# Two additive biases moved from VectorE and GpSimd into TensorE's accumulation, in a kernel of two transformer blocks

## The chip, the cores and the metric

The kernel runs on one core of a Trainium2 chip. The core has a matrix engine (TensorE, PE in the profile, whose weight loads stand in rows of their own as PEld), three engines for element work (VectorE or DVE, ScalarE or ACT, GpSimd or POOL), a queue engine that here only starts transfers (SyncE or SP), and 16 DMA engines. Each engine runs its own stream of instructions in order, and the streams meet at semaphores. The metric is the device time of one execution in microseconds: 2225.22 us, the median of 3 runs of the kernel before (2223.93 to 2225.47).

## The reference

256 tokens of width 2048 pass through two blocks in float32. Only two places of the first and second block matter here. In the first block a third of the mixer is a spatial gating unit: six heads, whose normalised values are mixed over the positions of a chunk of 128 and get a bias per head and position before they gate `u`:

```python
v = layernorm(v, ln_g, ln_b).reshape(B, L // CHUNK, CHUNK, N_GMLP_HEADS, GMLP_HEAD_DIM)
g = jnp.einsum('bnpec,eqp->bnqec', v, w_s) + b_s.T[:, :, None]
return u * g.reshape(B, L, D_GMLP)
```

The second block has causal attention of 16 heads of 128, with a bias on the logits that comes from forget gates, `cum[t]` being the running sum of their logarithms:

```python
log_f = jax.nn.log_sigmoid((f_pre + b_f).astype(jnp.float32)).transpose(0, 2, 1)
cum = jnp.cumsum(log_f, axis=-1)
logits = jnp.einsum('bhqd,bhkd->bhqk', q_i, k).astype(jnp.float32) * scale
logits = logits + c_i[..., :, None] - cum[..., None, :]
logits = jnp.where(pos_k[None, :] <= pos_q[:, None], logits, -jnp.inf)
p = jax.nn.softmax(logits, axis=-1)
```

The rest is eight large products with weight matrices (projections in and out, two feed-forward networks) with norms, convolutions and an FFT-like mixer between them.

## The kernel before

The weights come in 374 units of 1 MB. SP loads each into one of four buffers `raw` (L310). ACT rounds it to the short format fp32r into `whi` (L398), DVE subtracts to get the rest, `wlo` (L687); both have three buffers. PE multiplies each unit with the activations, which are split in the same way: 16 matmuls of 512 columns with `whi` (L1357) and 16 of 256 columns with `wlo` (L1368) for a unit of an input projection; 8 pairs with `whi` (L1392, L1393) and 8 with `wlo` (L1397) for a unit of an output projection. The units of the gated values and of the attention's values use L1360, L1361 and L1370. What DVE and ACT write beside, they write in the shadow of these products.

The order is written out by hand. A table `SIDE` says which small pieces of work an engine does behind which unit, and the engines go through the same table. `group` on ACT and DVE puts the pieces between the splits of the coming units; PE does them behind the unit's last matmul (`side(u)`).

The two places of the change:

**The gating unit.** `mix(j)`, j = 0 to 5. PE multiplies the normalised values of head j with its position matrix, once for each chunk of 128 (L1234), into one of the banks 4 to 7. DVE adds the bias from `bsb`, a row that a DMA has copied to all 128 partitions (L355), and writes `mb` (L832), then multiplies by the activated `u` into `actT` (L836). Heads 0 and 1 stand behind units 31 and 32, heads 2 and 3 behind unit 33, and heads 4 and 5 (`LAST_MIX`) right behind them. The next PE work is `rows(0)`, the output projection, whose first matmuls go to banks 4 and 5 and so wait until DVE has read heads 4 and 5 out of them. The last two blocks of `u` leave PE with unit 33 and pass through ACT (L441), DVE (L1083, L1086) and ACT's gelu (L605).

**The attention.** `sums` stands behind unit 194: PE multiplies the gate logarithms with a triangular matrix, once for the sums by head (L1326) and once by token (L1329); DVE copies them out as `cT` (16 heads by 256 positions, L912) and `ctok` (L914). POOL writes `cT` to DRAM (L366), reads it back into all 128 partitions by four DMAs (L369), and adds the causal mask for each head into `cbs` (L378, L379). `scores(h)` stands behind units 196, 200, up to 224, two heads at a time: PE multiplies queries and keys (L1249), the first 128 queries with 128 keys and the second 128 queries with 256. DVE adds `ctok` of the query and `cbs` of the key in one instruction per part (L928, L929) and takes the maximum (L931, L932); ACT does the exponential (L526, L527).

The kernel's functions that the change touches:

Of the kernel before, what the change touches and what calls it, by code (L numbers as in the profile page):

```python
# [120 lines left out]
def two_block_program(nc, A, out, cum):  # L121
    with ExitStack() as ctx:
        def sb(name, shape, dt=F):
            return ctx.enter_context(nc.sbuf_tensor(name, shape, dt))
# [18 lines left out]
        edge = sb("edge", [P, 64])  # L143
        bank = [ctx.enter_context(nc.psum_tensor(f"bank{i}", [P, 512], F)) for i in range(8)]
# [10 lines left out]
        def piece(q):  # L155
# [29 lines left out]
        bsb = view(5120, HY)  # L185
        mb = view(5888, 512, 2, T)
# [7 lines left out]
        qk = view(8192, 2048, 8, T)  # L194
        Sx = view(10496, 1536, 4, 384)
# [5 lines left out]
        cbs = view(17728, 768, 2, 384)  # L201
# [46 lines left out]
        s_gv, s_mean, s_nsq, s_napp, s_mix, s_mixb, s_mixd, s_gu, s_gelu, s_pg, s_pm, s_pd = (  # L248
            sem(n) for n in ("s_gv", "s_mean", "s_nsq", "s_napp", "s_mix", "s_mixb", "s_mixd", "s_gu", "s_gelu", "s_pg", "s_pm", "s_pd"))
# [3 lines left out]
        s_gf, s_xout, s_v, s_gt, s_ga, s_cum, s_cumd, s_qk0, s_qk, s_cbm, s_sc, s_scd, s_ex, s_dv, s_tp, s_pt, s_pv, s_pvt = (  # L253
            sem(n) for n in ("s_gf", "s_xout", "s_v", "s_gt", "s_ga", "s_cum", "s_cumd", "s_qk0", "s_qk", "s_cbm", "s_sc",
# [74 lines left out]
        def gpsimd(e):  # L329
# [25 lines left out]
            e.dma_start(bsb, A["gm_b_row"].partition_broadcast(P)).then_inc(s_bs, 16)  # L355
# [322 lines left out]
        def vector(e):  # L678
# [231 lines left out]
            def sums():  # L910
                e.wait_ge(s_cum, 2)
                e.tensor_scalar(cT, bank[5][0:16, 0:T], -1.0, None, ALU.mult).then_inc(s_cumd, 1)  # L912
                e.wait_ge(s_cum, 6)
                e.tensor_copy(ctok.rearrange("p (h c) -> p h c", h=2),  # L914
                              bank[4][:, 0:64].rearrange("p (h c) -> p h c", h=2)[:, :, 0:NH]).then_inc(s_cumd, 1)

            def scores(h):
                s, b = Sx[:, h % 4, :], 4 + h % 2
                mx = st[:, 22 + 2 * (h % 2):24 + 2 * (h % 2)]
                e.wait_ge(s_sc, h + 1)  # L920
                e.wait_ge(s_cumd, 2)
                e.wait_ge(s_cbm, 2 * h + 2)
                cb = cbs[:, h % 2, :]
# [4 lines left out]
                e.scalar_tensor_tensor(s[:, 0:P], bank[b][:, 0:P], ctok[:, h:h + 1], cb[:, 0:P], ALU.add, ALU.add).then_inc(s_scd, 1)  # L928
# [264 lines left out]
        def tensor(e):  # L1193
# [235 lines left out]
            rows(0, [in_free(18, 0), in_free(18, 1), in_free(17, 0), in_free(17, 1), (s_mixb, 5), (s_mixb, 6), (s_mixb, 3), (s_mixb, 4)])  # L1429
# [146 lines left out]
```

## Time and profile before

| | |
|---|---|
| median of 3 runs | 2225.22 us |
| the profiled execution | 2225.47 us |
| its span, first to last instruction | 2223.6 us |
| mean granted TensorE clock | 0.996 |
| PE busy | 2182.6 us, 98% of the span |
| PEld busy | 1871.3 us, 84% |
| DVE, ACT, POOL busy | 1306.7, 1013.5, 50.9 us |
| read from memory | 406.12 MB, 184 GB/s over the span |

The profile is of one execution. Busy time is the sum of an engine's instructions; the ends of matmuls are modelled, so a busy PE isn't one at its peak, and the distance between the starts of matmuls tells more than their length. One float32 matmul stands in the trace as two records, one fp32r matmul as one; both read "f32" in PE's rows.

### The profile page before, as it was taken

Reading aid. Unit: us, or ns where it says so; the run is one execution under the profiler, and the core shown is the slowest. Engines: PE = TensorE matmul, PEld = TensorE weight load, DVE = VectorE, ACT = ScalarE, POOL = GpSimd, SP = SyncE. Lnnn points to the kernel's source line nnn. Section 1 sums busy time; section 2 is a strip of 40 time slices with the busy share of each in tenths; the row PEclk is TensorE's granted clock in tenths of the full one; section 3 lists DMA queues with packets and bytes.
Section 4 is the critical chain, followed back from the end, with each engine's and each line's share of the span. In section 5 each row is a group of like instructions: output and inputs, shape, how many; then the busy total and the mean of one; then the engine's idle time right before and its main releaser. Section 6 shows DMA issues by size and latency. Waiting matters only on the chain.

```text
span 2223.6 us, 28008 instructions
## 1 busy us (share of the span) xinstructions
PE 2182.6 (98%) x11702; PEld 1871.3 (84%) x11702; DVE 1306.7 (59%) x1596; ACT 1013.5 (46%) x1227; POOL 50.9 (2%) x75
## 2 busy tenths in 40 slices
PE   7999999999999999999999999989999999999998
PEld 6888788888888888888898889878888888888886
DVE  7757647777777775444655665456555555444444
ACT  5444436545454554334654444444333334333333
POOL 1030000000000000000001000000000000000000
PEclk9999999999999999999999999999999999999999
DMA  9554555655555555555566555546666665555552
GB/s 303 159 159 152 197 189 177 210 189 187 188 188 188 188 189 189 190 190 187 155 191 200 161 171 190 190 132 192 188 188 189 190 189 189 190 189 189 189 189 95
DMA packets 267869, 410.04 MB, mean 184 GB/s; under 512 B 6629, under 2 KB 246309, under 8 KB 249312
## 3 DMA queue, kind: packets, MB, share of 16 engines
q1 hardware_dynamic: 264672, 395.47, 54.3%
q0 software_dynamic: 2352, 11.47, 1.4%
q8 instruction: 92, 1.51, 0.3%
q10 hardware_dynamic: 720, 1.32, 0.2%
q14 instruction: 33, 0.27, 0.0%
HBM read 406.12 MB, written 2.11 MB: 184 GB/s over the span
## 4 chain that ended last, share of the span: by engine, by line
PE 93%; DVE 2%; ACT 2%; issue 1%; DMA 1%; DVEq 0%; SPq 0%; ACTq 0%
PE bank L1357 33%; PE bank L1368 17%; PE bank L1392 11%; PE bank L1397 11%; PE bank L1393 11%; PE bank L1360 2%; PE bank L1361 2%; PE bank L1370 2%; DMA raw<-in_w_in 1%; ACT whi L398 1%; DVE wlo L687 1%; PE bank L1249 1%; PE bank L1203 1%; ACT M L416 0%; DVE M L1138 0%
## 5 line engine op out<-in xcount | busy, mean ns | idle before, releaser
L687 DVE TENSOR_TENSOR wlo<-raw,whi 128x2048 fp32r<-128x2048 f32 (+1 forms) x374 | 857.1, 2293 | 807.9 <-ACT whi L398 807.9
L398 ACT ACTIVATE whi<-raw 128x2048 fp32r<-128x2048 f32 (+1 forms) x374 | 715.8, 1916 | 823.8 <-PE bank L1397 442.8
L1357 PE MATMUL bank<-hh,whi 128*128 128x512 f32 x3392 | 825.4, 396 | 15.0 <-ACT whi L398 11.1
L1357 PEld LDWEIGHTS bank<-hh,whi 128*128 128x128 f32 x3392 | 626.6, 189 | 146.9 <-ACT whi L398 11.1
L1368 PEld LDWEIGHTS bank<-hh,wlo 128*128 128x128 f32 x3392 | 429.9, 188 | 17.3
L1368 PE MATMUL bank<-hh,wlo 128*128 128x256 f32 x3392 | 434.9, 281 | 0.0
L1392 PE MATMUL bank<-whi,hh 128*128 128x512 f32 x1088 | 428.8, 394 | 2.2 <-DVE M L832 2.2
L1393 PE MATMUL bank<-whi,hh 128*128 128x512 f32 x1088 | 427.5, 393 | 0.0
L1397 PE MATMUL bank<-wlo,hh 128*128 128x512 f32 x1088 | 274.3, 394 | 0.0
L1392 PEld LDWEIGHTS bank<-whi,hh 128*128 128x128 f32 x1088 | 204.5, 188 | 50.8 <-issue 2.4
L1397 PEld LDWEIGHTS bank<-wlo,hh 128*128 128x128 f32 x1088 | 204.3, 188 | 47.4
L1393 PEld LDWEIGHTS bank<-whi,hh 128*128 128x128 f32 x1088 | 204.5, 188 | 46.5
L459 ACT ACTIVATE M<-M,cols 128x256 f32<-128x256 f32 x106 | 58.0, 595 | 158.1 <-DVE M L768 158.1
L1360 PE MATMUL bank<-whi,hh 128*128 128x258 f32 (+1 forms) x352 | 88.3, 290 | 2.0 <-ACT whi L398 2.0
L1361 PE MATMUL bank<-whi,hh 128*128 128x258 f32 (+1 forms) x352 | 86.6, 285 | 0.0
L441 ACT ACTIVATE M<-bank 128x256 f32<-128x256 f32 x212 | 67.7, 371 | 19.1 <-PE bank L1368 9.6
L1360 PEld LDWEIGHTS bank<-whi,hh 128*128 128x128 f32 x352 | 67.7, 192 | 2.6 <-ACT whi L398 2.2
L1361 PEld LDWEIGHTS bank<-whi,hh 128*128 128x128 f32 x352 | 67.8, 193 | 0.4
L771 DVE SCALAR_TENSOR_TENSOR M<-M,cols 128x255 f32<-128x255 f32 x106 | 51.4, 484 | 18.2 <-ACT M L459 17.8
L754 DVE TENSOR_TENSOR hh<-M,hh 128x256 fp32r<-128x256 f32 x140 | 57.9, 419 | 4.4 <-ACT hh L438 4.4
L438 ACT ACTIVATE hh<-M 128x256 fp32r<-128x256 f32 x140 | 55.2, 400 | 6.6 <-PE bank L1368 3.4
L774 DVE SCALAR_TENSOR_TENSOR M<-M,cols 128x255 f32<-128x255 f32 x106 | 46.3, 479 | 0.0
(217 smaller groups left out, 893.1 us busy)
## 6 DMA issues: line engine op xcount, KB each, us to landing
raw<-in_mlp_w SPq DMA_DIRECT2D x128, 1024.0 KB, 5.4
raw<-in_ffn_w_up SPq DMA_DIRECT2D x88, 1024.0 KB, 5.0
raw<-in_ffn_w_down SPq DMA_DIRECT2D x44, 1024.0 KB, 4.7
raw<-in_w_in SPq DMA_DIRECT2D x34, 1024.0 KB, 5.5
raw<-in_fox_w_in SPq DMA_DIRECT2D x32, 1024.0 KB, 5.3
raw<-in_fox_w_in SPq DMA_DIRECT2D x16, 1032.0 KB, 5.5
raw<-in_w_out SPq DMA_DIRECT2D x16, 1024.0 KB, 4.8
raw<-in_fox_w_out SPq DMA_DIRECT2D x16, 1024.0 KB, 4.7
```

The costliest lines, as they stand in the source:

```text
L398: e.activation(whi[i % RING][:, 0:n], raw[i % RAW][:, 0:n], ACT.Copy).then_inc(s_hi, 1)
L441: return e.activation(dst, bank[b][:, T:2 * T], ACT.Copy)
L459: e.activation(dst, src, ACT.Identity, bias=bias, scale=ws[1]).then_inc(s_cv1, 1)
L687: e.tensor_tensor(wlo[i % RING][:, 0:n], raw[i % RAW][:, 0:n], whi[i % RING][:, 0:n].bitcast(F), ALU.subtract).then_inc(s_lo, 1)
L754: e.tensor_tensor(hlo[:, row_slot(stage, k), :], src[:, c, :], hhi[:, row_slot(stage, k), :].bitcast(F), ALU.subtract).then_inc(s_alo, 1)
L1357: e.matmul(bank[b][:, :], wh[:, k, s], hh[:, kk, :], start=kk == 0, stop=False)
L1360: e.matmul(o, hhi[:, kk, s], wh[:, k, :], start=kk == 0, stop=False)
L1361: e.matmul(o, hlo[:, kk, s], wh[:, k, :], start=False, stop=False)
L1368: t = e.matmul(bank[b][:, T:2 * T], wl[:, k, s], hhi[:, kk, :], start=False, stop=kk == KD - 1)
L1392: e.matmul(bank[b][:, :], hhi[:, s, h * P:h * P + P], wh[:, 512 * j:512 * j + 512], start=k == 0, stop=False)
L1393: e.matmul(bank[b][:, :], hlo[:, s, h * P:h * P + P], wh[:, 512 * j:512 * j + 512], start=False, stop=False)
L1397: t = e.matmul(bank[b][:, :], hhi[:, s, h * P:h * P + P], wl[:, 512 * j:512 * j + 512], start=False, stop=False)
```

## The change

The gating bias becomes a second matmul into the same bank: for each head and chunk PE multiplies a row of 128 ones (one partition) with the head's 128 biases (`bs6`, one partition, loaded by one small DMA), in float32. DVE's addition, `mb`, `bsb` and their semaphore go. Banks 4 to 7 are now free when DVE's multiplication by the activated `u` has been done.

The attention's key bias becomes a matmul too. DVE splits `cT` into an fp32r part and its rest and stacks them in `cs2`, partitions 0 to 15 and 32 to 47 of 64, which POOL has zeroed. For each head POOL multiplies `cs2` by a column `sel` that is one at the head's two rows and zero elsewhere, into `nck` (two buffers, fp32r); PE multiplies 64 rows of ones with it, 128 and 256 columns, behind each product of queries and keys. The way through DRAM and POOL's 32 additions go; DVE's additions read the mask itself. `sel` adds 16 columns to the packed constants.

```diff
@@ POOL @@
-            e.dma_start(bsb, A["gm_b_row"].partition_broadcast(P)).then_inc(s_bs, 16)
+            e.dma_start(bs6, A["gm_b_s"]).then_inc(s_bs, 16)
...
-            e.wait_ge(s_cumd, 1)
-            e.dma_start(cum[:, :], cT).then_inc(s_cdram, 16)
-            e.wait_ge(s_cdram, 16)
-            for n in range(4):
-                e.dma_start(actT[:, 4 * n:4 * n + 4, :].rearrange("p h t -> p (h t)"),
-                            cum[4 * n:4 * n + 4, :].rearrange("h t -> (h t)").partition_broadcast(P)).then_inc(s_cb[n], 16)
-            e.wait_ge(s_fox, 48)
+            e.memset(cs2, 0.0).then_inc(s_zero, 1)
+            e.wait_ge(s_cumd, 5)
             for h in range(NH):
-                b = cbs[:, h % 2, :]
-                if h % 4 == 0:
-                    e.wait_ge(s_cb[h // 4], 16)
                 if h >= 2:
-                    e.wait_ge(s_scd, 4 * (h - 2) + 2)
-                e.tensor_tensor(b[:, 0:P], actT[:, h, 0:P], msk[:, P:T], ALU.add).then_inc(s_cbm, 1)
-                e.tensor_tensor(b[:, P:384], actT[:, h, :], msk, ALU.add).then_inc(s_cbm, 1)
+                    e.wait_ge(s_sc, h - 1)
+                e.tensor_scalar(nck[:, h % 2, :], cs2, col("sel", h, 64), None, ALU.mult).then_inc(s_nck, 1)
@@ DVE, the gating unit @@
             def mix(j):
                 e.wait_ge(s_mix, j + 1)
-                e.wait_ge(s_bs, 16)
-                if j >= 2:
-                    e.wait_ge(s_mixd, j - 1)
-                e.tensor_tensor(mb[...], bank[4 + j % 4][:, 0:T]..., bsb[...]..., ALU.add).then_inc(s_mixb, 1)
-                e.wait_ge(s_mixb, j + 1)
                 e.wait_ge(s_gelu, j + 1)
-                e.tensor_tensor(actT[:, 10 + j, :], mb[:, j % 2, :], actT[:, 10 + j, :], ALU.mult).then_inc(s_mixd, 1)
+                e.tensor_tensor(actT[:, 10 + j, :], bank[4 + j % 4][:, 0:T], actT[:, 10 + j, :], ALU.mult).then_inc(s_mixd, 1)
@@ DVE, the attention @@
             def sums():
                 e.wait_ge(s_cum, 2)
                 e.tensor_scalar(cT, bank[5][0:16, 0:T], -1.0, None, ALU.mult).then_inc(s_cumd, 1)
+                e.wait_ge(s_cumd, 1)
+                e.tensor_copy(nck[0:16, 0, :], cT).then_inc(s_cumd, 1)
+                e.wait_ge(s_cumd, 2)
+                e.wait_ge(s_zero, 1)
+                e.tensor_copy(cs2[0:16, :], nck[0:16, 0, :].bitcast(F)).then_inc(s_cumd, 1)
+                e.tensor_tensor(cs2[32:48, :], cT, nck[0:16, 0, :].bitcast(F), ALU.subtract).then_inc(s_cumd, 1)
...
-                e.scalar_tensor_tensor(s[:, P:384], bank[b][:, P:384], ctok[:, NH + h:NH + h + 1], cb[:, P:384], ALU.add, ALU.add).then_inc(s_scd, 1)
+                e.scalar_tensor_tensor(s[:, P:384], bank[b][:, P:384], ctok[:, NH + h:NH + h + 1], msk, ALU.add, ALU.add).then_inc(s_scd, 1)
@@ PE @@
             def mix(j):
-                e.wait_ge(*((s_pd, j + 1) if j < 4 else (s_mixb, j - 3)))
+                e.wait_ge(*((s_pd, j + 1) if j < 4 else (s_mixd, j - 3)))
...
                 for n in range(2):
-                    t = e.matmul(bank[b][:, n * P:n * P + P], V[:, n, j * P:j * P + P], wsT[:, j, :], start=True, stop=True)
-                t.then_inc(s_mix, 1)
+                    o = bank[b][:, n * P:n * P + P]
+                    e.matmul(o, V[:, n, j * P:j * P + P], wsT[:, j, :], start=True, stop=False)
+                    t = e.matmul(o, ones[0:1, :], bs6[0:1, j * P:j * P + P], start=False, stop=True)
+                    if n:
+                        t.then_inc(s_mix, 1)
             def scores(h):
-                if h < 2:
-                    e.wait_ge(s_cumd, 2)
+                e.wait_ge(s_nck, h + 1)
...
                     w = P * (i + 1)
-                    t = e.matmul(bank[b][:, P * i:P * i + w], qT[:, i * P:i * P + P], kT[:, 0:w], start=True, stop=True)
-                t.then_inc(s_sc, 1)
+                    o = bank[b][:, P * i:P * i + w]
+                    e.matmul(o, qT[:, i * P:i * P + P], kT[:, 0:w], start=True, stop=False)
+                    t = e.matmul(o, onesr[0:64, :], nck[:, h % 2, 0:w], start=False, stop=True)
+                    if i:
+                        t.then_inc(s_sc, 1)
...
-            rows(0, [..., (s_mixb, 5), (s_mixb, 6), (s_mixb, 3), (s_mixb, 4)])
+            rows(0, [..., (s_mixd, 5), (s_mixd, 6), (s_mixd, 3), (s_mixd, 4)])
```

Three places show how the instructions stand. The first is PE at the end of the input projection, heads 4 and 5 of the gating unit and the start of the output projection; X holds the normalised values, M the activations and biases, hh the split activations. Before:

```order
L1234 MATMUL bank4<-X 128x128 [waits s_mixb]
L1234 MATMUL bank4<-X 128x128
L1234 MATMUL bank5<-X 128x128 [waits s_mixb]
L1234 MATMUL bank5<-X 128x128
L1392 MATMUL bank4<-whi1,hh 128x512 [waits s_mixb,s_alo,s_hi]
L1393 MATMUL bank4<-whi1,hh 128x512
L1392 MATMUL bank5<-whi1,hh 128x512 [waits s_mixb]
```

And after:

```order
L1224 MATMUL bank4<-X 128x128 [waits s_mixd]
L1225 MATMUL bank4<-M,ones 128x128
L1224 MATMUL bank4<-X 128x128
L1225 MATMUL bank4<-M,ones 128x128
L1224 MATMUL bank5<-X 128x128 [waits s_mixd]
L1225 MATMUL bank5<-M,ones 128x128
L1224 MATMUL bank5<-X 128x128
L1225 MATMUL bank5<-M,ones 128x128
L1386 MATMUL bank4<-whi1,hh 128x512 [waits s_mixd,s_alo,s_hi]
L1387 MATMUL bank4<-whi1,hh 128x512
L1386 MATMUL bank5<-whi1,hh 128x512 [waits s_mixd]
```

Each product is followed by one with the ones, and the output projection's first matmul in banks 4 and 5 waits for DVE's multiplication instead of its addition.

The second place is DVE at the same point, from heads 2 and 3 to heads 4 and 5. Before:

```order
L832 TENSOR_TENSOR M<-bank,M 128x256 [waits s_mixd,s_bs,s_mix]
L836 TENSOR_TENSOR M<-M 128x256 [waits s_gelu,s_mixb]
L1083 TENSOR_TENSOR M<-bank,M 128x256 [waits s_gus,s_unit]
L1083 TENSOR_TENSOR M<-bank,M 128x256 [waits s_gus]
L1086 TENSOR_TENSOR M<-M,rb 128x256 [waits s_gu] x2
L832 TENSOR_TENSOR M<-bank,M 128x256 [waits s_mixd,s_bs,s_mix]
L836 TENSOR_TENSOR M<-M 128x256 [waits s_gelu,s_mixb]
```

And after:

```order
L820 TENSOR_TENSOR M<-bank,M 128x256 [waits s_gelu,s_mix] x2
L1071 TENSOR_TENSOR M<-bank,M 128x256 [waits s_gus,s_unit]
L1071 TENSOR_TENSOR M<-bank,M 128x256 [waits s_gus]
L1074 TENSOR_TENSOR M<-M,rb 128x256 [waits s_gu] x2
L820 TENSOR_TENSOR M<-bank,M 128x256 [waits s_gelu,s_mix] x2
```

One instruction per head is left, and it waits for PE and for the gelu together.

The third place is PE at the first two heads of the attention, behind unit 196. Before:

```order
L1249 MATMUL bank4<-M 128x128 [waits s_cumd,s_qk]
L1249 MATMUL bank4<-M 128x256
L1249 MATMUL bank5<-M 128x128 [waits s_cumd,s_qk]
L1249 MATMUL bank5<-M 128x256
L1357 MATMUL bank0<-hh,whi2 128x512 [waits s_hi]
```

And after:

```order
L1241 MATMUL bank4<-M 128x128 [waits s_nck,s_qk]
L1242 MATMUL bank4<-nck,ones 128x128
L1241 MATMUL bank4<-M 128x256
L1242 MATMUL bank4<-nck,ones 128x256
L1241 MATMUL bank5<-M 128x128 [waits s_nck,s_qk]
L1242 MATMUL bank5<-nck,ones 128x128
L1241 MATMUL bank5<-M 128x256
L1242 MATMUL bank5<-nck,ones 128x256
```

Four matmuls for two heads have become eight, and the first of each head waits for POOL's `nck`.

## Rows read from the trace of the kernel before

**Rows 1.** The page: busy time by engine, and PE's clock in 40 slices.

```profile
PE 2182.6 (98%) x11702; PEld 1871.3 (84%) x11702; DVE 1306.7 (59%) x1596; ACT 1013.5 (46%) x1227; POOL 50.9 (2%) x75
...
PEclk9999999999999999999999999999999999999999
```

**Rows 2.** PE's waits over the span: who waited for whom, us, times, longest.

```profile
PE bank L1357 <- ACT whi L398: 11.1, 1, 11.1
...
PE bank L1392 <- DVE M L832: 2.2, 1, 2.2
```

**Rows 3.** PE in order of time around unit 196: start, length, line, operation.

```profile
1179.69 2.05 PE L1368 MATMUL bank<-hh,wlo 128*128 128x256 f32 x16
1181.57 1.48 PE L1249 MATMUL bank<-M 128*128 128x128 f32 x8
1182.70 4.01 PE L1357 MATMUL bank<-hh,whi 128*128 128x512 f32 x16
1186.55 2.04 PE L1368 MATMUL bank<-hh,wlo 128*128 128x256 f32 x16
1188.43 3.87 PE L1357 MATMUL bank<-hh,whi 128*128 128x512 f32 x16
```

**Rows 4.** The same at `sums`, behind unit 194.

```profile
1168.26 1.04 PE L1326 MATMUL bank<-M 128*16 128x256 f32 x4
1169.22 1.07 PE L1329 MATMUL bank<-M 128*128 128x16 f32 x8
1170.14 0.37 PE L1360 MATMUL bank<-whi,hh 128*128 128x258 f32 x1
```

**Rows 5.** The gating unit's end in order of time, on PE, DVE and ACT.

```profile
249.73 1.95 PE L1234 MATMUL bank<-X 128*128 128x128 f32 x16
...
250.38 0.42 DVE L832 TENSOR_TENSOR M<-bank,M 128x256 f32<-128x256 f32 x1 [1.21 <-PE bank L1234]
...
251.63 0.42 DVE L836 TENSOR_TENSOR M<-M 128x256 f32<-128x256 f32 x1
251.97 0.75 DVE L1083 TENSOR_TENSOR M<-bank,M 128x256 f32<-128x256 f32 x2
...
253.09 0.75 ACT L605 ACTIVATE M<-M 128x256 f32<-128x256 f32 x2 [2.50 <-DVE M L1086]
253.30 0.42 DVE L832 TENSOR_TENSOR M<-bank,M 128x256 f32<-128x256 f32 x1
253.87 0.47 PE L1392 MATMUL bank<-whi,hh 128*128 128x512 f32 x1 [2.19 <-DVE M L832]
...
254.57 0.51 PE L1392 MATMUL bank<-whi,hh 128*128 128x512 f32 x1
```

**Rows 6.** All instructions of the gating products, by line and form: count, busy us, mean ns.

```profile
L1234 PE MATMUL bank<-X 128*128 128x128 f32 x24 | 3.2, 274 | 0.0
```

**Rows 7.** DVE in order of time at `sums`.

```profile
1169.33 0.41 DVE L912 TENSOR_SCALAR M<-bank 16x256 f32<-16x256 f32 x1 [2.43 <-PE bank L1326]
1170.33 0.19 DVE L914 COPY M<-bank 128x32 f32<-128x32 f32 x1 [0.58 <-PE bank L1329]
```

**Rows 8.** POOL in order of time: the mixer's slowest operation, then the attention's bias.

```profile
153.75 3.07 POOL L350 TENSOR_TENSOR M<-M 128x384 f32<-128x384 f32 x1
1173.02 2.12 POOL L369 DMA_DIRECT2D M<-cum  x4 [2.48 <-DMA cum<-M]
1180.78 0.73 POOL L379 TENSOR_TENSOR M<-M 128x256 f32<-128x256 f32 x1
```

**Rows 9.** Waits between 1165 and 1365 us, all engines.

```profile
DVE M L928 <- PE bank L1249: 6.8, 8, 1.9
PEld bank L1249 <- DVE M L1119: 1.0, 4, 0.3
```

**Rows 10.** The start of the program on ACT, in order of time.

```profile
5.78 1.71 ACT L406 ACTIVATE hh<-X,cols 128x256 fp32r<-128x256 f32 x4 [3.10 <-DMA cols<-in_cols]
9.12 1.91 ACT L398 ACTIVATE whi<-raw 128x2048 fp32r<-128x2048 f32 x1 [1.63 <-DMA raw<-in_w_in]
```

More of the change, by code:

```diff
@@ L36 @@
 for _name, _n in (("mix", 16), ("ffn", 16), ("g0", 16), ("g2", 16), ("hyw", 54), ("hyb", 18), ("skip", 6),
-                  ("poolb", 4), ("pools", 4), ("ffw", 264), ("ffb", 88), ("gf", 16), ("filt", 4)):
+                  ("poolb", 4), ("pools", 4), ("ffw", 264), ("ffb", 88), ("gf", 16), ("sel", 16), ("filt", 4)):
     COLS[_name] = _at
@@ L118, in row_slot, with two_block_program @@
     return (k - ROWS[stage][1]) % 16
-def two_block_program(nc, A, out, cum):
+def two_block_program(nc, A, out):
     with ExitStack() as ctx:
@@ L143, in two_block_program @@
         edge = sb("edge", [P, 64])
+        nck = sb("nck", [64, 2, T], R)
         bank = [ctx.enter_context(nc.psum_tensor(f"bank{i}", [P, 512], F)) for i in range(8)]
@@ L184, in two_block_program @@
         wsT = Xf[:, 3072:3840].rearrange("p (e q) -> p e q", e=6)
-        bsb = view(5120, HY)
-        mb = view(5888, 512, 2, T)
+        bs6 = M[0:1, 5120:5888]
         fact = view(0, 44 * T, 44, T)
@@ L194, in two_block_program @@
         qk = view(8192, 2048, 8, T)
+        cs2 = M[0:64, 10240:10496]
         Sx = view(10496, 1536, 4, 384)
@@ L200, in two_block_program @@
         cT = M[0:16, 17408:17664]
-        cbs = view(17728, 768, 2, 384)
         ctok = view(17664, 2 * NH)
@@ L230, in two_block_program @@
             sem(n) for n in ("s_col", "s_id", "s_const", "s_decay", "s_fscale", "s_edge", "s_ln", "s_bs", "s_again", "s_fox"))
-        s_outd, s_outp, s_cdram = sem("s_outd"), sem("s_outp"), sem("s_cdram")
-        s_cb = [sem(f"s_cb{n}") for n in range(4)]
-        s_ones, s_pad = sem("s_ones"), sem("s_pad")
+        s_outd, s_outp = sem("s_outd"), sem("s_outp")
+        s_ones, s_pad, s_zero = sem("s_ones"), sem("s_pad"), sem("s_zero")
         s_hx, s_lx, s_sq, s_sumd, s_tot = (sem(n) for n in ("s_hx", "s_lx", "s_sq", "s_sumd", "s_tot"))
@@ L246, in two_block_program @@
         s_cv0, s_cvr, s_cv1, s_cv2, s_z, s_silu, s_fact = (sem(n) for n in ("s_cv0", "s_cvr", "s_cv1", "s_cv2", "s_z", "s_silu", "s_fact"))
-        s_gv, s_mean, s_nsq, s_napp, s_mix, s_mixb, s_mixd, s_gu, s_gelu, s_pg, s_pm, s_pd = (
-            sem(n) for n in ("s_gv", "s_mean", "s_nsq", "s_napp", "s_mix", "s_mixb", "s_mixd", "s_gu", "s_gelu", "s_pg", "s_pm", "s_pd"))
+        s_gv, s_mean, s_nsq, s_napp, s_mix, s_mixd, s_gu, s_gelu, s_pg, s_pm, s_pd = (
+            sem(n) for n in ("s_gv", "s_mean", "s_nsq", "s_napp", "s_mix", "s_mixd", "s_gu", "s_gelu", "s_pg", "s_pm", "s_pd"))
         s_ahi, s_alo, s_row, s_xsum = (sem(n) for n in ("s_ahi", "s_alo", "s_row", "s_xsum"))
-        s_gf, s_xout, s_v, s_gt, s_ga, s_cum, s_cumd, s_qk0, s_qk, s_cbm, s_sc, s_scd, s_ex, s_dv, s_tp, s_pt, s_pv, s_pvt = (
-            sem(n) for n in ("s_gf", "s_xout", "s_v", "s_gt", "s_ga", "s_cum", "s_cumd", "s_qk0", "s_qk", "s_cbm", "s_sc",
+        s_gf, s_xout, s_v, s_gt, s_ga, s_cum, s_cumd, s_qk0, s_qk, s_nck, s_sc, s_scd, s_ex, s_dv, s_tp, s_pt, s_pv, s_pvt = (
+            sem(n) for n in ("s_gf", "s_xout", "s_v", "s_gt", "s_ga", "s_cum", "s_cumd", "s_qk0", "s_qk", "s_nck", "s_sc",
                              "s_scd", "s_ex", "s_dv", "s_tp", "s_pt", "s_pv", "s_pvt"))
@@ L920, in scores @@
                 e.wait_ge(s_sc, h + 1)
-                e.wait_ge(s_cumd, 2)
-                e.wait_ge(s_cbm, 2 * h + 2)
-                cb = cbs[:, h % 2, :]
+                e.wait_ge(s_cumd, 5)
                 if h >= 4:
@@ L927, in scores @@
                     e.wait_ge(s_ex, 2 * h - 2)
-                e.scalar_tensor_tensor(s[:, 0:P], bank[b][:, 0:P], ctok[:, h:h + 1], cb[:, 0:P], ALU.add, ALU.add).then_inc(s_scd, 1)
-                e.scalar_tensor_tensor(s[:, P:384], bank[b][:, P:384], ctok[:, NH + h:NH + h + 1], cb[:, P:384], ALU.add, ALU.add).then_inc(s_scd, 1)
+                e.scalar_tensor_tensor(s[:, 0:P], bank[b][:, 0:P], ctok[:, h:h + 1], msk[:, P:T], ALU.add, ALU.add).then_inc(s_scd, 1)
+                e.scalar_tensor_tensor(s[:, P:384], bank[b][:, P:384], ctok[:, NH + h:NH + h + 1], msk, ALU.add, ALU.add).then_inc(s_scd, 1)
                 e.wait_ge(s_scd, 4 * h + 2)
@@ L1428, in tensor @@
                 mix(j)
-            rows(0, [in_free(18, 0), in_free(18, 1), in_free(17, 0), in_free(17, 1), (s_mixb, 5), (s_mixb, 6), (s_mixb, 3), (s_mixb, 4)])
+            rows(0, [in_free(18, 0), in_free(18, 1), in_free(17, 0), in_free(17, 1), (s_mixd, 5), (s_mixd, 6), (s_mixd, 3), (s_mixd, 4)])
             def up_free(g, n):
@@ L1542 @@
     ng = g["norm_g_2"][0]
+    sel = np.zeros((P, NH), np.float32)
+    sel[0:NH] = sel[32:32 + NH] = np.eye(NH)
     rows64 = np.zeros((P, 4), np.float32)
@@ L1548 @@
         cols(g["hy_skip"][0]), cols(g["pool_b"][0]), cols(g["pool_scale"][0]), cols(g["ffn_conv_w"][0]), cols(g["ffn_conv_b"][0]),
-        cols(g["norm_final"]), rows64], axis=1)
+        cols(g["norm_final"]), sel, rows64], axis=1)
     filt = np.zeros((64, 128), np.float32)
@@ L1571 @@
     out = nc.dram_tensor("out_0", (P, 2, D), F, kind="ExternalOutput").ap()
-    cum = nc.dram_tensor("cum", (NH, T), F, kind="Internal").ap()
-    two_block_program(nc, aps, out, cum)
+    two_block_program(nc, aps, out)
     r = run_bass_kernel_spmd(nc, [feeds], core_ids=[0])
```

6 lines of the change are left out of this document (2 added, 4 removed).

## The prediction

> **What bounds the kernel now.** I read the busy times first, then what PE waited for, then PE's order of time at the two places of the change. PE is busy for 2182.6 of 2223.6 us at full clock in every slice, the next engine, DVE, for 59% [rows 1]. PE's waits are few and single: 11.1 us at the start, then one or two at a seam between stages; of them only the 2.2 us of L1392 on DVE's L832 lies at a place that the change touches [rows 2]. In the attention's stretch PE's matmuls do not wait, but for four gaps in front of queries times keys that sum to 1.0 us on the weight loads and that DVE's L1119 ends, an instruction the change leaves alone; DVE's logits wait for PE and not for POOL [rows 9]. So PE's own instructions set the end, and whatever is added between them is paid, except where PE stands idle today. Work taken from DVE, POOL or the DMAs pays only where it shortens a PE wait.
>
> The measure for PE is the distance between starts. An fp32r matmul of 256 columns costs (1188.43 - 1186.55) / 16 = 0.1175 us [rows 3]. A float32 matmul is two records: the 12 gating products stand as 24 [rows 6]. Sixteen such records of 128 columns take 1.95 us, the last being 0.27 long, so (1.95 - 0.27) / 15 = 0.112 us each [rows 5]. Records of only 16 columns cost (1170.14 - 1169.22) / 8 = 0.115 us, and those of 256 columns (1169.22 - 1168.26) / 4 = 0.24 us [rows 4]. From 16 to 128 columns nothing changes; below 128 the weight load before each matmul sets the pace, at about 0.112.
>
> **The change part by part.** *The gating bias on PE.* 12 float32 matmuls of 128 columns are added, 24 records of 0.112 us = 2.7 us. Only the 8 records of heads 0 and 1, behind units 31 and 32, stand before units that are ready: 8 x 0.112 = 0.90 us on the path. The 16 records of heads 2 to 5 (1.79 us) stand ahead of PE's idle 2.19 us [rows 5] and fill it, so what they cost is how far that wait's end moves.
>
> *The wait's end.* Today: the products of heads 2 to 5 start at 249.73, DVE takes head 2 at 250.38, is done with head 3 at 251.63 + 0.42, turns to the two blocks of u at 251.97 (the trace lets neighbours overlap a little), ACT's gelu starts 1.12 us later, at 253.09, and the first L832 behind it at 253.30; PE starts bank 4 at 253.87 and bank 5 at 254.57 [rows 5]. After: head 3's last product is the 16th record, not the 8th, and ends near 249.73 + 15 x 0.112 + 0.27 = 251.68. DVE has one instruction for it, 251.73 to 252.15, so the blocks of u start at about 252.17, 0.20 later, and the gelu at 253.29. The multiplication of head 4 must now wait for the gelu of its block: 253.29 + 0.38 + 0.05 = 253.7 to 254.15, with PE 0.15 behind it, at 254.30, and its third matmul, the first in bank 5, two matmuls further, at 254.30 + 0.31 + 0.23 = 254.84 (head 5's multiplication ends at 254.60, before that). Against 254.57 this is +0.27 us. PE's own queue, full until 249.73 + 31 x 0.112 + 0.27 = 253.5, is not the last. Behind PE stands the whole output projection, behind DVE the split of unit 36, which waits for ACT anyway (ACT's split follows the gelu by 0.1 us) and is needed 10 us later.
>
> If heads 2 to 5 were not hidden at all this term would be +1.79; if the saved additions of heads 2 and 3 (0.84 us) moved the wait's end forward in full, -0.6.
>
> *The attention's bias on PE.* For each of 16 heads two fp32r matmuls, of 128 and of 256 columns. The 256-column one is of the same kind as L1368: 0.1175. No row has an fp32r matmul of 128 columns. From below: half of 0.1175, 0.06, if columns alone count. From above: 0.225, the two records of 0.112 that float32 takes, if the short matmul gets no benefit from its format. I take 0.112, the floor that the 16-column records show. Sum 16 x (0.112 + 0.1175) = 3.67 us, with ends 16 x 0.1775 = 2.8 and 16 x 0.3425 = 5.5. All of it is on the path: these stand between two units whose whi and wlo are ready, with no idle time before or behind them [rows 3].
>
> The Trainium skill ("TensorE: Matmul & The Clock Gate", Back-to-back issue gap) gives 81 ns for a sustained matmul of 128 columns with its weight load. The 0.112 of rows 5 contradicts it for float32. By that figure the estimate for all additions would be 8 x 0.081 + 0.27 + 16 x (0.081 + 0.1175) = 4.1 us instead of 4.8.
>
> *DVE, POOL and the wait on nck.* `sums` gets three instructions of 16 partitions by 256. At 0.41 each as L912 [rows 7] plus a semaphore between them, the last ends near 1169.74 + 3 x 0.43 = 1171.0, `ctok` at 1171.2, and the split behind it starts 0.8 us later; its unit is needed near 1182. POOL then makes nck for heads 0 and 1. Nearest rows: 0.73 us for 128x256, up to 3.07 for 128x384 [rows 8]. Even 3.07 each ends by 1177.4, while PE comes to head 0 at 1181.57 [rows 3]. Later pairs have some 25 us. Cost zero, hidden under unit 195 and 196; the cover ends at (1181.57 - 1171.2) / 2 = 5.2 us for each POOL instruction. The trip through DRAM that goes had landed at 1180.0, before PE came: it wins nothing. DVE's logits start later by the two or four added matmuls, 0.46 us for a pair; the exponentials and splits behind them finish more than 4 us before PE's next unit, so this is not seen.
>
> *Constants and DMA.* `cols` grows by 16 of 522 columns, 3% of a transfer that lands before 5.78 us; the first unit's weights, which land at 9.12, gate PE [rows 10]. The removed broadcasts were not waited for by PE. Both zero, within 0.1.
>
> **Sum.** 0.90 + 0.27 + 3.67 = +4.84 us. The profiled execution took 2225.47 us, which is 0.25 above the median of 2225.22; from its own time the sum gives 2230.3, from the median 2230.1. I take 2230.1, +0.22%. What a measurement of this kernel can tell from no change is about 0.2%, here 4.45 us; the forecast is only just over it.
>
> **Rivals.** *A, not slower: the weight load isn't the floor for the new matmuls.* The 64 rows of ones are fp32r; if their load is quicker than a float32 one, the 128-column matmuls stream at 0.06 and the attention's term is 2.84. Sum 0.90 + 0.27 + 2.84 = 4.0, 2229.2 us, +0.18%: no change. For it: no row has an fp32r load that isn't covered by 256 columns. Against: the 16-column floor, and 0.1175 for 256 columns lies above the 0.107 of streaming at 2.4 GHz, so even there something is added for the load. It decides at 0.088 us for the short matmul, where the total is 4.45.
> The Trainium skill (the same page, Weight-path perf modes) says that fast weight load applies to 128 weights of a type other than FP32. If the chip counts fp32r as another type, that is rival A; no row here shows it.
>
> *B: short fp32r matmuls cost as float32.* Then the attention's term is 5.48 and the time 2225.2 + 6.65 = 2231.9, +0.30%. For it: no product of the kernel uses fp32r under 256 columns, so no row excludes it. Against: float32 itself reaches 0.112 for a record of 128 columns, and one record of fp32r has no reason in the rows to take longer than one of float32.
>
> *C: POOL becomes the wait.* If a multiplication by a column takes 8 us for 64 partitions, nck of head 1 comes 16 us after 1171.2 and PE waits 5.6 us once: 2235.7. Against: 3.07 is the longest POOL row.
>
> *D, faster: PE gets its pace back.* If the 2 MB of broadcast and POOL's additions disturbed PE's reads, their removal would speed up the matmuls around. It would need more than 4.84 us of some 180 us of attention. Against: the 256-column matmuls of unit 196, during the broadcast's aftermath and POOL's additions, take (1181.57 - 1179.69) / 16 = 0.1175, as those of unit 197 when neither runs [rows 3]. Where it holds, a time of 2224 or less.
>
> **How the numbers follow.** My forecast has 0.55, A 0.17, B 0.20, C 0.04, D 0.04. Around 4.84 the two added places and the run-to-run spread of a median leave about 0.8 us either way, so the forecast itself gives slower by over 0.2% in two of three cases, 0.36, and no change in 0.19. A gives no change, 0.12, and slower 0.05; B and C slower, 0.24; D no change or faster, half each. Together faster 0.02, no change 0.34, slower 0.64; I shift a little for what no row shows: 0.03, 0.35, 0.62. The range runs from A less its spread, 2227.4, to B plus its spread, 2232.9.
>
> **What would show it.** In the profile after, L1242's records of 128 and 256 columns stand 0.11 and 0.12 us before the next start; a distance of 0.06 is A, of 0.22 is B. The pair of heads behind unit 196 takes 1.13 + 0.46 = 1.6 us from its start to the next unit's. L1225 has 24 records at 0.112. The wait of L1386 on DVE shrinks from 2.19 to about 0.8 us (254.30 against the end of PE's queue at 253.5) and ends 0.4 us later than today, counted from head 2's first product; if it ends 1 us later, that step is wrong. POOL's tensor_scalar is under 1 us and no PE wait names it. I am wrong altogether if PE's waits elsewhere change by more than 1 us.

## The result, and the profile after

The changed kernel takes 2248.2 us in the median of four runs (2247.5 to 2249.1), the kernel before 2225.3 (2223.9 to 2226.6). The ratio is 1.0102, with a 95% interval of 1.0087 to 1.0118: slower by 22.9 us, where 4.9 were forecast. The profiled executions took 2247.4 and 2225.5 us, their spans are 2244.9 and 2223.6 us. The working below is made against these spans, +21.3 us; that is 1.6 less than between the medians, and the four runs of the kernel before alone lie 2.7 us apart.

The page after: busy time by engine, and PE's clock in 40 slices.

```profile
PE 2206.8 (98%) x11758; PEld 1883.9 (84%) x11758; DVE 1306.1 (58%) x1593; ACT 1013.3 (45%) x1227; POOL 46.5 (2%) x55
...
PEclk9999999999999999999999999999999999999999
```

Against [rows 1], PE has 56 records more, as the change has it (24 gating records, 32 attention matmuls), and 24.2 us more busy time. That is 0.43 us for each record, where 0.11 to 0.12 were forecast. DVE and ACT are busy for as long as before, within 0.6 us, and POOL for 4.4 us less.

PE's longest waits in the span after: who waited for whom, us, times, longest.

```profile
PE bank L1351 <- ACT whi L388: 10.9, 1, 10.9
PE bank L1191 <- DVE X L1132: 7.1, 3, 5.0
PE bank L1197 <- DVE M L716: 3.4, 1, 3.4
PE bank L1354 <- ACT whi L388: 2.1, 1, 2.1
PE bank L1351 <- DVE M L755: 1.4, 1, 1.4
```

The 2.2 us of L1392 [rows 2] are gone altogether, and the rest stands as it was, within 0.6 us. So no wait was added: the time is inside PE's own sequence. PE in order of time, at the first pair of heads behind unit 196:

```profile
1189.01 0.39 PE L1241 MATMUL bank<-M 128*128 128x128 f32 x2
1189.32 0.33 PE L1242 MATMUL bank<-nck,ones 64*128 64x128 f32 x1
1189.58 0.70 PE L1241 MATMUL bank<-M 128*128 128x256 f32 x2
1190.21 0.38 PE L1242 MATMUL bank<-nck,ones 64*128 64x256 f32 x1
1190.52 0.49 PE L1241 MATMUL bank<-M 128*128 128x128 f32 x2
1190.94 0.32 PE L1242 MATMUL bank<-nck,ones 64*128 64x128 f32 x1
1191.19 0.70 PE L1241 MATMUL bank<-M 128*128 128x256 f32 x2
1191.82 0.38 PE L1242 MATMUL bank<-nck,ones 64*128 64x256 f32 x1
1192.13 0.74 PE L1351 MATMUL bank<-hh,whi 128*128 128x512 f32 x2
```

The pair took 1.13 us [rows 3] and takes 3.12, not 1.6. The bias matmuls of 64 rows are not the only ones that have become dear: from an L1242 to the next L1241 it is 0.26 to 0.31 us, and the two records of an L1241 of 256 columns behind it take 0.63 us up to the next start, where they took 0.43. The weight loads show what happens, first a pair of before, then the changed kernel (same columns, the bracket is idle time):

```profile
1181.46 1.19 PEld L1249 LDWEIGHTS bank<-M 128*128 128x128 f32 x8
```

```profile
1188.89 0.31 PEld L1241 LDWEIGHTS bank<-M 128*128 128x128 f32 x2
1189.32 0.18 PEld L1242 LDWEIGHTS bank<-nck,ones 64*128 64x128 f32 x1
1189.58 0.30 PEld L1241 LDWEIGHTS bank<-M 128*128 128x128 f32 x2
1190.21 0.18 PEld L1242 LDWEIGHTS bank<-nck,ones 64*128 64x128 f32 x1 [0.33 <-issue]
```

Before, the eight loads of a pair ran one behind the other, beside the matmuls ahead of them. Now the weight load engine is idle ahead of each load of an L1242, and waits for nothing that the profile can name: for 0.12 us behind the loads of a product of 128 columns, for 0.33 us behind those of one of 256 columns. The longer gap comes 16 times and sums to 5.3 us. The gaps stand where the number of weight rows changes, and they are longer where the matmul ahead is longer, as if the load waited for that matmul to end.

The gating products of heads 2 to 5, the same view (rows between repeat):

```profile
252.01 0.39 PE L1224 MATMUL bank<-X 128*128 128x128 f32 x2
252.33 0.48 PE L1225 MATMUL bank<-M,ones 1*128 1x128 f32 x2
252.74 0.49 PE L1224 MATMUL bank<-X 128*128 128x128 f32 x2
253.16 0.48 PE L1225 MATMUL bank<-M,ones 1*128 1x128 f32 x2
...
258.60 0.79 PE L1225 MATMUL bank<-M,ones 1*128 1x128 f32 x2
259.32 0.80 PE L1386 MATMUL bank<-whi,hh 128*128 128x512 f32 x1
```

Four records cost 0.83 us instead of 4 x 0.112 = 0.45: 0.19 more for each of the two changes. From head 2 to the output projection it was 4.14 us with 2.19 of them idle [rows 5]; now it is 7.31 with none. And at the end the clock falls. Windows, before the fall and in it (length; busy time with count of PE, PEld, DVE, ACT, POOL; granted clock; DMA share; GB/s):

```profile
252.00:257.30 5.30, 5.30 (x28) 3.74 (x26) 2.18 (x6) 1.16 (x4) 0.00 (x0) 1.00 0.40 165
257.50:263.10 5.60, 5.60 (x15) 4.16 (x15) 3.20 (x4) 2.15 (x3) 0.55 (x1) 0.50 0.37 102
```

From 257.5 us the clock is at half, 1.2 GHz, for 6.8 us, right behind a stretch in which PE was busy all the time at 2.4 GHz.

Where the 21.3 us are: I set the starts of ACT's splits, unit by unit, against those of before. The difference is -0.25 at unit 34 (the start), 7.5 from unit 37 on, flat to unit 198, 22.6 at unit 228 and 21.2 from unit 250 on. So the gating brings 7.7 us, the attention 15.1, and at the seam behind it 1.3 come back: there the clock is at half in one piece of 6.8 us that PE waits through in part (busy 4.8), and not in two of 3.4 (busy 6.5 together). By an estimate, half of the busy time at half clock is lost, 2.4 against 3.2 us, and PE's wait on DVE's hh is 0.6 us shorter. So these 1.3 us go with where the clock falls and not with the new matmuls; the runs set side by side under "The gating part again" bear this out.

### The profile page after: what moved, and what is told of

Its sections match the earlier page's. It is cut to its first block, busy times and chain, and to the rows that moved or that the text cites. A ratio compares the mean times of both kernels' runs of the same rounds, so it can differ in the third digit from the quotient of the medians.

```text
span 2244.9 us, 28087 instructions
## 1 busy us (share of the span) xinstructions
PE 2206.8 (98%) x11758; PEld 1883.9 (84%) x11758; DVE 1306.1 (58%) x1593; ACT 1013.3 (45%) x1227; POOL 46.5 (2%) x55
## 4 chain that ended last, share of the span: by engine, by line
PE 94%; DVE 2%; ACT 2%; issue 1%; DMA 1%; DVEq 0%; SPq 0%; ACTq 0%
PE bank L1351 33%; PE bank L1362 17%; PE bank L1386 11%; PE bank L1391 11%; PE bank L1387 11%; PE bank L1354 2%; PE bank L1355 2%; PE bank L1364 2%; DMA raw<-in_w_in 1%; ACT whi L388 1%; DVE wlo L677 1%; PE bank L1241 1%; PE bank L1191 0%; PE bank L1242 0%; ACT M L406 0%
## 5 line engine op out<-in xcount | busy, mean ns | idle before, releaser
L1351 PE MATMUL bank<-hh,whi 128*128 128x512 f32 x3392 | 825.1, 396 | 14.0 <-ACT whi L388 10.9
L1351 PEld LDWEIGHTS bank<-hh,whi 128*128 128x128 f32 x3392 | 626.5, 189 | 145.9 <-ACT whi L388 10.9
L1386 PE MATMUL bank<-whi,hh 128*128 128x512 f32 x1088 | 430.6, 396 | 0.0
L1386 PEld LDWEIGHTS bank<-whi,hh 128*128 128x128 f32 x1088 | 205.5, 189 | 48.6 <-issue 0.2
L431 ACT ACTIVATE M<-bank 128x256 f32<-128x256 f32 x212 | 67.7, 371 | 20.3 <-PE bank L1362 10.9
```

The costliest lines, as they stand in the source:

```text
L431: return e.activation(dst, bank[b][:, T:2 * T], ACT.Copy)
L1351: e.matmul(bank[b][:, :], wh[:, k, s], hh[:, kk, :], start=kk == 0, stop=False)
L1386: e.matmul(bank[b][:, :], hhi[:, s, h * P:h * P + P], wh[:, 512 * j:512 * j + 512], start=k == 0, stop=False)
```

## The experiments

In what follows "H" is the theory that each change of the number of weight rows that the array works with makes PE wait for the matmul ahead before it loads, and "T" that small-row matmuls are slow in themselves. "S" blames the second matmul into the same region of a bank, and "F" the change between float32 and fp32r. Offsets are those of ACT's splits against before, as above.

**One part at a time.** The gating part alone (e1), the attention part alone (e2), each by giving back the other part's lines of before:

```
 e1:  t = e.matmul(bank[b][:, P*i:P*i + w], qT[...], kT[:, 0:w], start=True, stop=True)    # as before
 e2:  t = e.matmul(bank[b][:, n*P:n*P + P], V[...], wsT[:, j, :], start=True, stop=True)   # as before
```

> Only the gating part of the change, the attention as before. Theory H (a change of the number of weight rows between neighbouring matmuls, 128 to 1 and back, lets PE finish and load before it goes on, some 0.2 us each way): 1.1 us more for each of heads 0 and 1, about 2.7 us for heads 2 to 5 beyond the wait they fill, and about 3.4 us of half clock behind them: +7 to +8 us. Rival S (a second matmul into the same bank region right behind the first is what waits): the same here, +7 to +8.

> Only the attention part, the gating unit as before. All theories: 8 pairs of heads at 1.9 us more each, +15 us, less about 1.3 us that the seam behind the attention gave back in the changed kernel: +14 us.

e1: 2233.07 us, ratio 1.0029 (1.0019 to 1.0039). In its profiled run the offset goes from -0.3 to 8.9 at the gating and stays, above the 7 to 8 expected; the clock is at half from 255.6 us for 10.2 us, longer than in the whole change. e2: 2241.85 us, 1.0066 (1.0051 to 1.0081); from -0.1 at unit 198 to 15.1 at unit 228, 13.8 behind the seam. Against the 2226.35 us of before beside them that is 6.7 and 15.5 us in the medians, 22.2 together, where the whole change has 22.9: as far as these medians can tell, the parts add up and don't work on each other.

**The same with 128 rows.** In e3 the gating bias, in e4 the attention bias is multiplied on all 128 rows, the rows added being zeros. Number and length of matmuls stay. e9 is the whole change in this form.

```
-  t = e.matmul(o, ones[0:1, :], bs6[0:1, j * P:j * P + P], start=False, stop=True)
+  t = e.matmul(o, ones, bs6[:, j * P:j * P + P], start=False, stop=True)        # e3, e9
-  t = e.matmul(o, onesr[0:64, :], nck[:, h % 2, 0:w], start=False, stop=True)
+  t = e.matmul(o, onesr[0:128, :], nck[:, h % 2, 0:w], start=False, stop=True)  # e4, e9
```

> As the gating part alone, but the ones and the biases have 128 rows, row 0 the biases and the others zero, so that every matmul has 128 weight rows; same count, columns and format. Theory H: each record back to 0.112 us, no fall of the clock, +0.9 for heads 0 and 1 and up to 0.3 at the wait: +1.2 us. Rival S (same bank region) : unchanged, +7 to +8. Rival F (float32 next to something else) can't apply, both are float32.

> As the attention part alone, but cs2, sel, nck and the ones have 128 rows, the added ones zero. Theory H: the 128-column matmul at 0.112 and the 256-column one at 0.1175, +0.46 us for a pair of heads, +3.7 us in all. Rival F (the alternation of float32 and fp32r is what waits): unchanged, +14. Rival S (same bank region): unchanged, +14.

> The whole change with 128 rows for every matmul of the ones, in both places (zeros below the rows in use). Theory H: the sum that the prediction made for matmuls without any change of row count, +1.0 at the gating unit and +3.7 in the attention, +4.7 us, 2230 us. If something else of the change cost time, it would lie above +6.

e3: 2225.76 us, ratio 0.9998 (0.9989 to 1.0008); the medians can't tell 1 us from nothing, so the order of time has to. The gating adds 1.04 us, from -0.47 to +0.57. PE in order of time at its end:

```profile
253.31 0.39 PE L1231 MATMUL bank<-X 128*128 128x128 f32 x2
253.54 0.39 PE L1232 MATMUL bank<-M,ones 128*128 128x128 f32 x2
254.72 0.47 PE L1391 MATMUL bank<-whi,hh 128*128 128x512 f32 x1 [0.79 <-DVE M L831]
```

The distance is 0.223 for two records, 0.112 each; PE waits 0.79 us where 0.8 were forecast; the clock does not fall. The second matmul into the same region of a bank is still there, so S falls.

e4: 2230.99 us, 1.0015 (1.0006 to 1.0025); 3.76 us from unit 198 to 228, forecast 3.67. The products are float32 and the biases fp32r, as in e2, so F falls too. e9: 2230.78 us against 2225.58, 1.0022 (1.0013 to 1.0031), which is the forecast's 1.0022. Its offset rises by 1.0 at the gating and 3.7 in the attention, and PE stands in the pair so:

```profile
1182.52 0.39 PE L1243 MATMUL bank<-M 128*128 128x128 f32 x2
1182.66 0.30 PE L1244 MATMUL bank<-nck,ones 128*128 128x128 f32 x1
1182.81 0.65 PE L1243 MATMUL bank<-M 128*128 128x256 f32 x2
...
1184.29 2.02 PE L1353 MATMUL bank<-hh,whi 128*128 128x512 f32 x8
```

1.77 us, where the 64 rows took 3.12. Rows of zeros make the kernel faster by 17 us: the count of matmuls was priced rightly, and what was missed hangs on the row number alone.

**How many rows.** e5 takes 96 rows, e6 takes 32 (the low part of the key's bias is left out, since it doesn't fit).

```
-  t = e.matmul(o, onesr[0:64, :], nck[:, h % 2, 0:w], ...)
+  t = e.matmul(o, onesr[0:96, :], nck[:, h % 2, 0:w], ...)     # e5;  onesr[0:32, :] in e6
```

> The attention part alone, with cs2, sel, nck and the ones on 96 rows instead of 64 (the rows above 48 are zero); gating as before. Theory H1 (what matters is the part of the array that a matmul occupies, and 96 rows occupy all of it as 128 do): +3.7 us in the attention, pairs of heads at +0.46. Theory H2 (any difference in the number of rows makes PE finish first): as with 64 rows, +15 us, pairs at +1.9.

> The attention part alone on 32 rows; the low part of the key bias is left out for that (rows 32 to 47 don't exist), so the logits miss it. H1 and H2: a third size of the occupied part, again different from 128, +15 us. A theory in which the price falls or grows with the rows missing: 64 rows cost 1.43 us per pair over the matmuls themselves; 96 missing rows instead of 64 would make it 2.1 and the total about +21 us.

e5: 2229.25 us against 2226.77, 1.0012 (1.0002 to 1.0023), 3.65 us in the attention: as with 128. e6: 2241.23 us, 1.0067 (1.0047 to 1.0087), 15.3 us: as with 64. PE in order of time in e5:

```profile
1182.84 0.39 PE L1244 MATMUL bank<-M 128*128 128x128 f32 x2
1182.98 0.31 PE L1245 MATMUL bank<-nck,ones 96*128 96x128 f32 x1
...
1184.61 0.64 PE L1354 MATMUL bank<-hh,whi 128*128 128x512 f32 x2
```

So not every other number of rows has a price. 96 is as good as 128; 64 and 32 cost, both the same. This fits an array that is used in another division for 64 rows or fewer; the division itself stands in no row.

**Fewer changes, same matmuls.** In e7 two heads are done together, the four products first and then their biases, so that a pair has 4 changes and not 8. The order, with the waits ahead of a pair that it needs, is the only difference to e2.

```
+  for k, q, kk in ((h, qT, kT), (h + 1, qk[:, sl + 1, :], qk[:, sl + 3, :])):
+      e.matmul(bank[4 + k % 2][...], q[...], kk[:, 0:w], start=True, stop=False)
+  for k in (h, h + 1):
+      t = e.matmul(bank[4 + k % 2][...], onesr[0:64, :], nck[:, k % 2, 0:w], start=False, stop=True)
```

> The attention part alone with 64 rows, the two heads of a pair interleaved: two products of queries and keys, then two with the ones, twice. The same matmuls, but 4 changes of the row count per pair instead of 8. Theory H (each change costs some 0.18 us, whatever stands between): 0.46 + 4 x 0.18 = 1.2 us per pair, +9.4 us in the attention. Rival T (each 64-row matmul is slow in itself, 0.36 us each): unchanged, 1.9 per pair, +15 us.

2237.85 us, 1.005 (1.0033 to 1.0066); 11.8 us in the attention. T, which wanted 15, falls; but 9.4 isn't met either. PE in order of time at the first and the second pair of heads:

```profile
1181.32 0.61 PE L1246 MATMUL bank<-M 128*128 128x128 f32 x4
1181.86 0.43 PE L1248 MATMUL bank<-nck,ones 64*128 64x128 f32 x2
1182.22 1.13 PE L1246 MATMUL bank<-M 128*128 128x256 f32 x4
1183.28 0.51 PE L1248 MATMUL bank<-nck,ones 64*128 64x256 f32 x2
1183.72 0.50 PE L1357 MATMUL bank<-hh,whi 128*128 128x512 f32 x1
...
1208.62 0.71 PE L1246 MATMUL bank<-M 128*128 128x128 f32 x4 [0.38 <-DVE M L1114]
```

The first pair takes 2.40 us: 1.77 + 4 x 0.16. The rest is a side effect of the edit: both heads' queries and keys must now be there before the first starts, and PE waits for DVE's copy L1114 (the L1119 of before) 11 times, 4.6 us in all, where it was 4 times and 1.0. I summed the distance from a pair's first product to the next unit's first matmul over the eight pairs:

| kernel | changes | distance, us | over e4, per change |
|---|---|---|---|
| before | 0 | 9.50 | |
| e4, 128 rows | 0 | 14.69 | |
| e5, 96 rows | 0 | 14.72 | |
| e7, 64 rows, in fours | 32 | 19.89 | 0.163 |
| e6, 32 rows | 64 | 25.45 | 0.168 |
| after, 64 rows | 64 | 25.48 | 0.169 |

The price for each change is the same in all three, and T falls on this table alone: the same matmuls take 5.6 us less with half the changes. From unit to unit, as the offsets count, a change costs a little more, 0.177 us; the rest comes in the unit behind. With 3.7 + 32 x 0.163 and 2 to 3.6 us of added waiting (part of it ran beside matmuls still queued) e7 should show 10.9 to 12.5; it shows 11.8.

**The kernel before had the same cost.** Its filter products at L1282 have 64 rows. e10 puts them on 128, with zeros, in the kernel before:

```
-  t = e.matmul(bank[b][:, 0:384], fe[:, m*P:m*P + P], w3[:, ...], start=True, stop=True)                    # M[0:64, ...]
+  t = e.matmul(bank[b][:, 0:384], M[:, 17664 + m*P:17664 + m*P + P], M[:, 9728 + ...], start=True, stop=True)
```

> The kernel before, untouched but for the filter's third product: its weights and data get 128 rows instead of 64, the added ones zero (16 records in two blocks, so 4 changes of the row count go). Theory H: about 0.2 us for each change, -0.8 us in two steps of 0.4 behind units 7 and 10, too little for the time of the whole to show. If the rows of the kernel before were slow there for another reason: no step.

2224.68 us, 0.9994 (0.9986 to 1.0003): too little for a median. But the order of time shows it. Before, then e10, around the first of two such blocks, with the unit behind it:

```profile
59.84 2.08 PE L1368 MATMUL bank<-hh,wlo 128*128 128x256 f32 x16
61.85 2.84 PE L1282 MATMUL bank<-M 64*128 64x384 f32 x8
64.63 2.56 PE L1357 MATMUL bank<-hh,whi 128*128 128x512 f32 x10
...
68.39 2.04 PE L1368 MATMUL bank<-hh,wlo 128*128 128x256 f32 x16
```

```profile
59.58 2.08 PE L1373 MATMUL bank<-hh,wlo 128*128 128x256 f32 x16
61.51 2.74 PE L1287 MATMUL bank<-M 128*128 128x384 f32 x8
63.98 3.26 PE L1362 MATMUL bank<-hh,whi 128*128 128x512 f32 x13
...
67.76 2.05 PE L1373 MATMUL bank<-hh,wlo 128*128 128x256 f32 x16
```

e10 is ahead by 0.26 us in front of the block, and by 0.63 behind it: 0.37 for two changes. Behind the second block it is 1.03, and it stays about there up to unit 36. Four changes, 0.19 each, in another stage, another type of work and without the change under study.

**Everything but the bias matmuls.** e8 leaves both kinds of bias matmul out and keeps all the rest of the change.

```
-  e.matmul(o, V[...], wsT[:, j, :], start=True, stop=False)
-  t = e.matmul(o, ones[0:1, :], bs6[0:1, ...], start=False, stop=True)
+  t = e.matmul(o, V[...], wsT[:, j, :], start=True, stop=True)      # likewise the one on nck
```

> The changed kernel with the matmuls of the ones left out in both places, so that both biases are missing from the output; DVE, POOL and the DMAs are as changed. What the rest of the change is worth: all theories expect the PE wait at the output projection to end some 0.5 us earlier, since DVE's additions are gone, and nothing else: -0.5 us, no change. If freed DVE, POOL or DMA work gave PE back some of its pace (the former rival D), it would be faster by more than 1 us.

2224.96 us, 0.9994 (0.9984 to 1.0003). The offset falls by 0.8 us between units 35 and 36, where 0.5 were expected and the wait on DVE shrinks from 2.2 to 1.7, and is flat in the attention. What DVE, POOL and the DMAs were relieved of pays there and nowhere else.

**The gating part again.** e11 is e1 once more, for the clock.

> The gating part alone once more, one look for the clock. If the drawn-out matmuls of heads 2 to 5 bring the clock down, the half clock stands behind 253 us again, for 6.8 us or more, as in the changed kernel and in the first run of this one. If it was chance, 3.4 us or none, as in the runs with the gating unit of before.

2234.95 us in a single run; 7.7 us at the gating; the clock is at half from 259.8 us for 6.8 us. The lengths at half clock at the end of the gating, over the profiled runs of all kernels here:

| gating | kernels | at half clock, us |
|---|---|---|
| with 1-row biases | after, e11 | 6.8 |
| with 1-row biases | e1 | 10.2 |
| as before | before, e2, e7 | none |
| as before | e4, e5, e6, e10 | 3.4 |
| 128-row biases | e3, e9 | none |
| without the bias matmuls | e8 | none |

Three of three against none or one of the shortest kind. That the drawn-out stretch brings the longer fall is likely from this. Why the clock falls where it does, and why in four of the seven with the gating of before, was not settled.

What a fall costs can be read from the same runs. The 3.4 us at half clock in e4, e5, e6 and e10 stand in a gating unit that was not changed, and the offset rises there by 1.3 to 1.5 us. At the seam behind the attention the offset falls by 1.3 us in every kernel that has one piece of 6.8 us and no other (after, e2, e4, e6, e10, the last without any change in the attention), and moves by 0.1 at most where two pieces of 3.4 us stand as before (e1, e3, e9, e11). So a kernel's time moves by more than 1 us with the place of these pieces alone.

## Why the prediction was wrong

*The step that failed* is the price of PE's new matmuls: "From 16 to 128 columns nothing changes; below 128 the weight load before each matmul sets the pace, at about 0.112", and with it "8 x 0.112" and "16 x (0.112 + 0.1175)". I priced columns and type and took the number of rows as free. All rows I took the price from were of 128 rows. The bounds came from the same rows, so the range could not hold the time either.

What the runs showed in its place: beside the price of each matmul, each change of the weight rows, there or back, costs 0.16 to 0.20 us, and there are 88 of them, 64 in the attention and 24 in the gating unit.

- *Gating, heads 0 and 1:* forecast 0.90; the products of head 2 start 2.28 us later against before, 2.53 with the earlier start. 0.90 + 8 changes x 0.20.
- *Gating, heads 2 to 5:* forecast +0.27 with a wait of 0.8 left. The wait is gone: with 0.83 us for each product PE's queue alone would end at 252.01 + 0.73 + 7 x 0.83 = 258.6 at full clock, later than DVE. That is 2.4 us; the fallen clock adds 0.8 up to L1386 and some 2 behind it.
- *Attention:* forecast 3.67, measured 15.1 = 3.76 + 64 x 0.177.
- *The clock:* not foreseen at all; nearly 3 us of the gating's 7.7.

In sum 2.5 + 2.4 + 2.8 + 15.1 - 1.3 (seam) - 0.25 (start) = 21.3 us.

*What stood in the trace before.* The 16 records of L1368 take 1.88 us up to a product of 128 rows [rows 3] and 2.01 up to the 64 rows of L1282 (59.84 to 61.85 above); the 8 records of L1282 take 2.78 us to the next unit, in e10 2.47 (both in the lines above). I had not looked for rows with fewer than 128 weight rows, though both added matmuls have them. At `sums` the number of weight columns changes, from 128 to 16 and back, and [rows 4] show 0.24 us for a record of 256 columns; I read this as the price of columns. That reading was not quite right. Record by record, L1326 stands 0.216 us apart, as the records of 256 columns with 128 weight columns do (L1313 to L1316, around 185 us), and only the last one is 0.31 us ahead of L1329. So that change of columns seems to cost 0.09 us, half of a change of rows. It is one place, and no run tried it by itself.

*The rule that was missed.* The Trainium skill has it, in "TensorEngine Tiling (Array Packing)", Tiling Modes, Key Properties: "Mode switching requires drain: Changing tiling mode (not just tile) drains the TensorE". The modes it lists in the same section have 128, 64 or 32 rows. The runs agree: 64 and 32 rows cost the same and 96 nothing, as if 96 rows ran in the mode of 128, and the load behind a change starts late. The page gives no price; here it is 0.16 to 0.20 us. That PE empties itself first is the page's account; the rows show the distances and the late loads, not the inside of the array.

*What held.* With 128 rows the working comes out term by term (e3: 1.04 against 0.90 + 0.27, wait 0.79 against 0.8, its end 0.39 us later than today against 0.4; e4: 3.76 against 3.67; e9: 1.0022). The pair alone was to take 1.6 and takes 1.77, but unit to unit it is 0.47, as summed; the difference returns in the unit behind. In the attention DVE, POOL and the DMAs cost and bring nothing (e8). POOL's first nck starts at 1178.58, which less the 7.5 of shift is the 1171.1 forecast, and the first two are ready 6.6 us ahead of PE. The first takes 2.9 us and not less than 1, as forecast, but it is hidden:

```profile
1178.58 3.80 POOL L369 TENSOR_SCALAR nck<-M,cols 64x256 fp32r<-64x256 f32 x2 [60.13 <-DVE M L904]
1190.69 0.92 POOL L369 TENSOR_SCALAR nck<-M,cols 64x256 fp32r<-64x256 f32 x1 [8.30 <-PE bank L1242]
```

*The rivals.* A and B are settled by e4: if the long one costs its 0.1175, 3.76 / 16 - 0.1175 = 0.118 us are left for a short fp32r matmul, not 0.06 and not 0.225. C did not happen (0.92 us each, 3.8 for the first two together). D is refuted by e8: without the added matmuls the attention's offset is flat. None of them spoke of the row number.

*Slips in the working.* Neither changes the outcome. With the 0.8 us of spread that the prediction states, its range would start at 2228.4 and not at 2227.4. The parts of "slower" add up to 0.65 and those of "no change" to 0.33, not 0.64 and 0.34.

## What to carry to other kernels

Before a matmul with fewer than 128 weight rows is put between full ones, look in the trace for a place where the row number changes already, and price each crossing, there and back, beside the matmul itself; here filling up with zeros to 128 rows (in the attention 96 were enough) cost nothing that shows and took 17 us of 23 away. Where small-row matmuls can't be padded, put them together, and count the waits that the new order brings (e7 saved half of the changes and gave 2 to 3.6 us of waiting back). And take the bounds of a new instruction from rows that share each of its sizes; a bound from rows that differ in one of them bounds nothing.

## What the runs showed of the hardware

- A change from 128 weight rows to 64, 32 or 1, or back, costs PE 0.16 to 0.20 us, as a mean of the two directions, with fp32r (e2, e6, e7) and float32 (e1, e10) in the small matmuls and at 128 to 384 columns; 96 rows count as 128 (e5).
- It is paid by the full matmuls around as well, so a view by line does not show it. Only distances between starts do (0.63 us instead of 0.43 for the L1241 of 256 columns above).
- PE reads as fully busy while this goes on: 5.30 of 5.30 us in the window above. A busy share of 98% did not mean that PE was at its pace.
- An fp32r matmul of 128 columns at 128 rows costs about 0.118 us, as much as the 0.1175 of 256 columns (an estimate from e4 and e9, from unit to unit).
- 3.4 us at half clock, with PE busy, cost 1.3 to 1.5 us of the whole (e4, e5, e6, e10 behind unit 36).
